# Feed-forward stages of a two-block transformer forward pass: weight blocks multiplied two at a time, on four PSUM banks

## The reference

```python
def conv_ffn(h, w_up, conv_w, conv_b, w_down):
    u = causal_dwconv(h @ w_up, conv_w, conv_b)      # 3 taps over the tokens
    g, v = jnp.split(u, 2, axis=-1)
    return (jax.nn.gelu(g, approximate=True) * v) @ w_down

h = rmsnorm(x, ffn_norm[layer])                       # x: 256 x 2048
x = x + conv_ffn(h, ffn_w_up[layer], ...)             # w_up 2048 x 12288, w_down 6144 x 2048
```

## Time and profile before

| | us |
|---|---|
| median of 3 runs | 3134.07 (3133.66 to 3134.08) |
| span of the profiled execution, first to last instruction | 3131.4 |
| PE busy | 3108.4 (99%) |
| DVE busy | 2315.0 (74%) |
| ACT busy | 1650.6 (53%) |
| granted TensorE clock, mean | 0.999 of full speed |

### The profile page before, as it was taken

The page is one execution under the profiler, slowest core; times in us unless marked ns, Lnnn a source line. Parts: engine busy times, 40 slices in busy tenths (PEclk is TensorE's granted clock), DMA queues, the critical chain, the costliest instruction groups (busy, mean ns, idle before and its releaser), DMA issues.

```text
span 3131.4 us, 52278 instructions
## 1 busy us (share of the span) xinstructions
PE 3108.4 (99%) x18922; PEld 2770.3 (88%) x18922; DVE 2315.0 (74%) x3605; ACT 1650.6 (53%) x2203; POOL 8.0 (0%) x12
## 2 busy tenths in 40 slices
PE   8999999999999999999999999999999999999998
PEld 7988888888888899988888888888898888888887
DVE  7877886787688778888866876878677777666665
ACT  5664554554455457755544544554446654444444
POOL 1000000000000000000000000000000000000000
PEclk9999999999999999999999999999999999999999
DMA  6335555555555645565555555555434455544443
GB/s 222 124 128 186 189 187 201 177 189 197 181 191 178 210 160 182 176 227 176 188 200 177 190 196 183 189 190 197 168 134 162 162 180 183 174 164 171 174 171 138
DMA packets 80334, 561.55 MB, mean 179 GB/s; under 512 B 9424, under 2 KB 10448, under 8 KB 13136
## 3 DMA queue, kind: packets, MB, share of 16 engines
q1 hardware_dynamic: 80208, 559.87, 51.2%
HBM read 557.73 MB, written 2.10 MB: 179 GB/s over the span
## 4 chain that ended last, share of the span: by engine, by line
PE 98%; DVE 1%; ACT 0%; DMA 0%; issue 0%; POOL 0%; DVEq 0%; SPq 0%; ACTq 0%
PE unit L317 50%; PE unit L320 26%; PE s L317 3%; PE s L320 1%; PE unit L540 1%; PE unit L590 1%; PE unit L592 1%; PE unit L591 1%; PE unit L542 1%; PE unit L541 1%; PE o L411 1%; PE tr L592 0%; PE tr L591 0%; PE tr L590 0%; PE unit L711 0%; PE v L317 0%
## 5 line engine op out<-in xcount | busy, mean ns | idle before, releaser
L1368 DVE TENSOR_TENSOR w_tail<-raw,w_head 128x2048 fp32r<-128x2048 f32 (+1 forms) x532 | 1207.5, 2271 | 140.0 <-ACT w_head L909 137.3
L909 ACT ACTIVATE w_head<-raw 128x2048 fp32r<-128x2048 f32 (+1 forms) x532 | 1011.2, 1901 | 496.1 <-DMA raw<-in_up 137.4
L317 PE MATMUL unit<-h,w_head 128*128 128x512 f32 x4912 | 1196.1, 392 | 0.0
L317 PEld LDWEIGHTS unit<-h,w_head 128*128 128x128 f32 x4912 | 902.8, 188 | 175.7
L320 PE MATMUL unit<-h,w_tail 128*128 128x256 f32 x4912 | 665.7, 284 | 0.0
L320 PEld LDWEIGHTS unit<-h,w_tail 128*128 128x128 f32 x4912 | 632.7, 191 | 18.4 <-issue 0.3
L1377 DVE TENSOR_TENSOR prod<-unit,lo 128x256 f32<-128x256 f32 x436 | 184.6, 423 | 391.3 <-ACT lo L916 389.4
L317 PE MATMUL unit<-act,w_head 128*128 128x512 f32 x1920 | 469.3, 391 | 0.0
L916 ACT ACTIVATE lo<-unit 128x256 f32<-128x256 f32 x436 | 166.8, 383 | 533.6 <-PE unit L320 518.5
L317 PEld LDWEIGHTS unit<-act,w_head 128*128 128x128 f32 x1920 | 353.2, 188 | 69.7
L320 PE MATMUL unit<-act,w_tail 128*128 128x256 f32 x1920 | 263.6, 283 | 0.0
(11 more groups left out here) (306 smaller groups left out, 2897.7 us busy)
## 6 DMA issues: line engine op xcount, KB each, us to landing
raw<-in_up SPq DMA_DIRECT2D x192, 1024.0 KB, 4.8
raw<-in_down SPq DMA_DIRECT2D x96, 1024.0 KB, 4.8
raw<-in_odd SPq DMA_DIRECT2D x64, 1024.0 KB, 4.8
raw<-in_even_b SPq DMA_DIRECT2D x32, 1024.0 KB, 4.8
raw<-in_attn SPq DMA_DIRECT2D x24, 1024.0 KB, 4.9
raw<-in_wo SPq DMA_DIRECT2D x16, 1024.0 KB, 4.8
raw<-in_lru_x SPq DMA_DIRECT2D x16, 1024.0 KB, 4.8
raw<-in_lru_y SPq DMA_DIRECT2D x16, 1024.0 KB, 4.8
```

What stands on the lines that cost most here:

```text
L317: pe.matmul(bank[:, :], w_head[:, slot, k * P:(k + 1) * P], src[:, k, :], start=k == 0, stop=False)
L909: a.activation(w_head[:, slot, 0:width], raw[:, r, 0:width], ACT.Copy).then_inc(head_done, 1)
L1368: v.tensor_tensor(w_tail[:, slot, 0:width], raw[:, slot % 2, 0:width], w_head[:, slot, 0:width].bitcast(F32), ALU.subtract).then_inc(tail_ ...
```

## The change

In up and down stages, all units but the first two of a stage (the first two of each stage stay single units) go two at a time through a new function `pair`: 16 H of the one block, 16 H of the next, 16 T of the one, 16 T of the next, on two banks. The four units of a loop turn take the four banks unit0, unit1, s0, s1. ACT and DVE read their results from the bank of the unit; their order of work, and all semaphores' counts, are as before.

```diff
@@ build
         out_bank = {"wo": score_bank, "lru_out": wide_bank, "even_out": score_bank, "odd_out": score_bank}
+        out_bank.update((f"{kind}{layer}{r}", score_bank) for kind in ("up", "down") for layer in range(2) for r in range(ROUNDS))
@@ tensor
+            def pair(u, slot, src):
+
+                for s in range(2):
+                    bank = score_bank[slot + s]
+                    pe.wait_ge(head_done, u + s + 1)
+                    pe.wait_ge(bank_free, u + s - LEAD)
+                    for k in range(KT):
+                        pe.matmul(bank[:, :], w_head[:, slot + s, k * P:(k + 1) * P], src[:, k, :], start=k == 0, stop=False)
+                for s in range(2):
+                    bank = score_bank[slot + s]
+                    pe.wait_ge(tail_done, u + s + 1)
+                    for k in range(KT):
+                        last = pe.matmul(bank[:, 0:SEQ], w_tail[:, slot + s, k * P:(k + 1) * P], src[:, k, 0:SEQ],
+                                         start=False, stop=k == KT - 1)
+                    last.then_inc(unit_done, 1)
+
             def plain(name, src, ready=None, norm=None):
 
                 def body(i):
-                    for j in range(RING):
-                        first = known(i) and j == 0
-                        unit(i * RING + (BASE[name] + j), j, src, ready=ready if first else None, norm=norm if first else None)
+                    u = i * RING + BASE[name]
+                    if known(i):
+                        unit(u, 0, src, ready=ready, norm=norm, own=(score_bank[0], u - LEAD))
+                        unit(u + 1, 1, src, own=(score_bank[1], u + 1 - LEAD))
+                    else:
+                        pair(u, 0, src)
+                    pair(u + 2, 2, src)
                 repeat(pe, 0, UNITS[name] // RING, body)
@@ scalar, up
-                        step(i * RING + (BASE[name] + j), j, r == 0 and known(i) and i == 0 and j == 0)
+                        step(i * RING + (BASE[name] + j), j, r == 0 and known(i) and i == 0 and j == 0, bank=score_bank[j])
@@ vector, up
-                        product(u, j)
+                        product(u, j, score_bank[j])
```

## The result

The changed kernel takes 3140.87 us (median of 13 runs, 3140.48 to 3141.77), the kernel before 3133.74 (13 runs beside it, 3133.36 to 3134.69): 7.1 us or 0.23% slower, ratio 1.0023 with a 95% interval of 1.0016 to 1.0031. The forecast was +7.8 us and 3141.9.

What follows compares the result with a forecast made beforehand. PE, busy 99% of the span, was taken to bound the kernel. Waits of 9.6 and 1.0, less 2.6 for matmul order and 0.2 for banks, gave +7.8 us: 3141.9 us, range 3136.5 to 3149.

Steps and rivals of the forecast that it cites:

- Waits for `act`: At six up-to-down changes, PE waits 1.6 us each at k = 15 of the down stage's first unit: +9.6 us.
- Waits for `acc`: After `down02` and `down12`, PE waits 0.5 us each for the sum of squares: +1.0 us for both.
- Order of matmuls: In up and down stages, each of 132 pairs saves one H-T turn of 0.02 us: -2.6 us.
- Four banks: Near the start of `down12`, PE's one short wait for a bank goes: -0.2 us.
- A: At the stage's end the wait doesn't appear, so the kernel is not slower: 3131.3 us; chance 0.10.
- B: PE starves in every pair of the up stages as loads delay each other: 27 us more, 3169; chance 0.07.
- C: Clock falls to 1.2 GHz behind each of eight new waits, 5.6 us each: 45 more, 3187; chance 0.03.

Runs made afterwards that it cites:

- the two halves: Changed kernel with one list reordered at up stages' ends: DVE's alone (block 33's tail later) 3140.50 us; ACT's alone (block 34's head later) 3139.63 us.
- mending them: Changed kernel, all pairs kept; at up stages' ends DVE makes block 33's tail and ACT block 34's head later: 3132.29 us.
- all ends mended: Changed kernel with DVE's and ACT's lists reordered at up stages' ends, and DVE's tail of the next stage's third block later in `down02` and `down12`: 3131.03 us.
- single ends and late heads: Changed kernel with the last two units of each up stage single, and ACT making the heads of blocks 33 and 34 later: 3145.55 us.
- my own first mend: Changed kernel with the last two units of each of the six up stages single again: 3137.06 us.

## Why the prediction was right, step by step

- **Waits for `act`.** Right in place and number: six, from unit 30's later end, with DVE's and ACT's lists both in the way, which the two halves and their sum show. Size: the first unit of `down01` is 7.13 - 5.65 = 1.48 us longer, forecast 1.6. I had `act` at +6.76, it came at +6.62, and the signal took 0.05, not 0.1. The forecast has `act` late because it adds rows by their ends, which run into the next row's start by some 0.1 us; besides, its sum for DVE, -1.30 + 4.01, is +2.71 and not +2.75, which changes nothing since ACT's path gave +2.76. So k = 15 starts only 1.37 us later than before. The other 0.1 I had not counted: behind the stop that matmul is longer, 0.50 us for 0.40, and its T follows 0.34 behind it in place of 0.24. The two errors lie opposite ways, so that the size comes this close is in part luck. Six make 8.9; mending them gave 8.6.
- **Waits for `acc`.** Right, two. DVE's `product` of unit 15 in `down02` is at 1105.85 - 1102.80 = +3.05 (forecast 2.94), and PE's matmul behind it at +5.22 where it was at +4.69:

```profile
1102.80 0.28 PE L611 MATMUL unit<-h,w_head 128*128 128x256 f32 x1
...
1105.85 0.42 DVE L1398 TENSOR_TENSOR prod<-s,lo 128x256 f32<-128x256 f32 x1
...
1107.55 0.42 DVE L1424 TENSOR_TENSOR acc<-acc,sq 128x256 f32<-128x256 f32 x1
...
1108.02 0.70 PE L360 MATMUL norm<-acc,ones 128*128 128x256 f32 x2 [0.38 <-DVE acc L1424]
```

  That is 0.53, forecast 0.5. Behind `down12` it is 0.62, since before PE came to that matmul at +4.59 there; the forecast took 4.69 for both. Mending both gave 3132.29 - 3131.03 = 1.3: here too 0.1 follows each stop, so they cost a little more than the 1.0 forecast.
- **Order of matmuls.** Right: 0.02 us per pair, 11.13 to 11.11, and the 15 pairs of `up01` make its 0.29. In the kernel with all ends mended every up stage is 0.30 us shorter than before, and every down stage but `down12` 0.14 to 0.15; that is 2.6 for 132 pairs. By the medians, with no wait left, pairs against the same banks without pairs give 3133.39 - 3131.03 = 2.4 us, forecast 2.6. That 32 T in a row would make the next H run dearer did not happen.
- **Four banks.** -0.2, forecast -0.2: the medians alone could not tell it, the 0.17 of `down12` in the traces does.
- **Together**: 8.9 + 1.3 - 2.6 - 0.2 = 7.4 beside 7.1 of the medians. The profiled spans differ by 8.1; 0.6 of that are the two old waits, which were longer in that execution.
- **Rivals.** A, no wait at the end: refuted. B, starving in every pair: no wait inside a stage. But half of it was true. B reckoned with the load behind the odd unit's tail, which does land in time. The one behind the even unit's tail it left out, and ACT waits 2.3 us for that one in every pair, where before it waited 0.6 to 1.3 in every unit. This costs PE nothing in a pair and came out only where single units followed. C, the clock: in the changed kernel it stays at its upper level, with a mean of 0.999 over the execution. But C's mechanism exists: in the kernel with single ends and late heads the clock fell behind one of its eight stops, at 1.6 us and not the 5.6 that C reckoned with.

What the prediction got wrong is outside the change itself: my own first mend, single units at the ends, failed since I counted only when unit 30 ends and not what stands ahead of its copy.

## What to carry to other kernels

When work is reordered inside a stage whose consumers run far behind, cost it at the stage's end, where the consumer's last result is asked for at once: count what stands in each in-order list ahead of the last copies, and compare with the slack there (here 0.68 us against a shift of 2.0). If two lists stand in the way, as here, mending one can be worth almost nothing, so a change that brings nothing alone is not yet refuted. Put work for later blocks behind the last results of a stage, on all engines together: moved on one alone, it can become a new wait for the next.

## What the runs showed of the hardware

- A run of 512-column matmuls starts a little slower behind a run of 256-column ones: its first five follow each other at 228 to 236 ns in place of 227, 0.027 us in all, whether 16 or 32 of the narrow ones came before. The other way round the first narrow one is 7 ns early. Both together are the 0.02 us that a pair saves.
- A change of PSUM bank with two semaphore waits that are already met costs nothing between equal matmuls: in a pair the first H of the second block starts 227 ns behind the last of the first, like all others.
- A stop of 1.21 us in PE's list of waits lengthens its unit by 1.48. Of the rest, 0.16 is that the row of the matmul ahead runs on for 0.28 us where the next one normally starts after 0.12, and 0.10 that the matmul behind the stop is longer.
- The granted clock stayed at 2.4 GHz through the six stops of 1.2 us in the changed kernel, and through one of 2.18 us in another, but fell to 1.2 GHz for 3.4 us behind one of 1.82 us there. The mean of the execution, 0.998, does not tell this; the rows of the stretch do.
